# Attention: the order of the compressed parts of tiles 4 to 7, and the oldest key tile of tile 4's selected part

## The reference, cut to what matters

```python
o_cmp, o_sel = map_query_blocks(
    lambda q, p: nsa_cmp_sel(q, p, kc, vc, c_end, ks_b, vs_b, m_ov, rel_bias), (q_a,), pos)
...
o_win = window_attend(q_a..., band(kv_a[:, :, 4]), band(kv_a[:, :, 5]), k_pos, rel_bias)
o_lat = map_query_blocks(lambda ql, qr, p: mla_attend(ql, qr, ckv, k_rope, p, pos), (q_lat, q_rope), pos)
...
o_a = gates[..., 0:1] * o_cmp + gates[..., 1:2] * o_sel + gates[..., 2:3] * o_win
```

## Time and profile before

| | |
|---|---|
| median of 3 runs | 1113.71 us (1111.62 to 1114.09) |
| profiled execution | 1115.21 us |
| its span | 1113.2 us |
| busy: TensorE, VectorE, ScalarE, GpSimd | 1075.2, 624.6, 362.5, 86.5 us |
| granted TensorE clock, mean | 0.991 of 2.4 GHz |
| attention of the prompt | from about 386 to 753 us |

### The profile page before, as it was taken

The page is one execution under the profiler, slowest core; times in us unless marked ns, Lnnn a source line. Parts: engine busy times, 40 slices in busy tenths (PEclk is TensorE's granted clock), DMA queues, the critical chain, the costliest instruction groups (busy, mean ns, idle before and its releaser), DMA issues. The chain is left out here.

```text
span 1113.2 us, 22587 instructions
## 1 busy us (share of the span) xinstructions
PE 1075.2 (97%) x8368; PEld 763.3 (69%) x8368; DVE 624.6 (56%) x1627; ACT 362.5 (33%) x893; POOL 86.5 (8%) x184
## 2 busy tenths in 40 slices
PE   6899999999999999998999999999999999999997
PEld 3455599998886677776776657664544576777775
DVE  0645323463423477769677766742323588888883
ACT  0322001121112475546555555631112133333330
POOL 0210100110000011101101010011000200000000
PEclk9899999999999999999999999999999999999998
DMA  9933270001006240000000000005794467878781
GB/s 355 310 115 94 72 211 2 16 19 72 1 1 122 44 116 2 1 1 2 1 2 1 2 1 2 1 1 119 169 307 152 142 217 262 271 274 275 261 251 51
DMA packets 96612, 120.25 MB, mean 108 GB/s; under 512 B 31569, under 2 KB 65380, under 8 KB 95480
## 3 DMA queue, kind: packets, MB, share of 16 engines
q1 hardware_dynamic: 96504, 118.81, 34.4%
HBM read 104.41 MB, written 14.36 MB: 107 GB/s over the span
## 5 line engine op out<-in xcount | busy, mean ns | idle before, releaser
L549 PE MATMUL PS<-AR 128*128 128x256 f32 (+2 forms) x896 | 219.7, 403 | 0.0
L549 PEld LDWEIGHTS PS<-AR 128*128 128x128 f32 x896 | 167.8, 190 | 45.2 <-issue 6.2
L2090 PE MATMUL PS<-AR 128*128 128x512 f32 x256 | 112.3, 592 | 0.0
L1747 PE MATMUL PS<-CA,AR 128*128 128x128 f32 x704 | 111.4, 282 | 0.8 <-ACT AR L1821 0.8
L963 DVE TENSOR_TENSOR AR<-PS,AR 128x256 f32<-128x256 f32 (+2 forms) x80 | 36.2, 452 | 134.4 <-PE PS L549 134.3
L1747 PEld LDWEIGHTS PS<-CA,AR 128*128 128x128 f32 x704 | 77.0, 143 | 44.6 <-issue 31.7
L1821 ACT ACTIVATE AR<-PS 128x512 f32<-128x512 f32 (+1 forms) x108 | 58.2, 546 | 125.1 <-PE PS L1747 124.5
L1725 PE MATMUL PS<-AR 128*128 128x65 f32 (+1 forms) x688 | 89.3, 271 | 0.0
L2090 PEld LDWEIGHTS PS<-AR 128*128 128x128 f32 x256 | 47.5, 190 | 54.0 <-issue 54.0
L1725 PEld LDWEIGHTS PS<-AR 128*128 128x128 f32 x688 | 84.3, 192 | 0.0
L1806 ACT ACTIVATE AR<-PS,SM_ 128x512 f32<-128x512 f32 (+4 forms) x192 | 76.6, 471 | 15.9 <-DVE SM_ L1914 8.8
(11 more groups left out here) (364 smaller groups left out, 1622.9 us busy)
## 6 DMA issues: line engine op xcount, KB each, us to landing
AR<-in_cache_nsa SPq DMA_DIRECT2D x128, 256.0 KB, 5.0
AR<-in_cache_mla SPq DMA_DIRECT2D x128, 96.0 KB, 3.7
AR<-in_x_prompt SPq DMA_DIRECT2D x16, 512.0 KB, 4.6
AR<-in_w_ada SPq DMA_DIRECT2D x3, 2048.0 KB, 11.4
AR<-in_w_in SPq DMA_DIRECT2D x6, 1024.0 KB, 8.4
AR<-in_w_ada SPq DMA_DIRECT2D x8, 512.0 KB, 4.3
AR<-in_w_out SPq DMA_DIRECT2D x4, 1024.0 KB, 10.0
AR<-in_w_out SPq DMA_DIRECT2D x2, 2048.0 KB, 17.5
```

The lines of the kernel that those rows point to most:

```text
L549: mm = pe.matmul(bank[:, 0:WIDE[g]], tokens[:, k, :], w, start=(fresh and k == 0), stop=(last and k == 3), skip_group_check=True)
L1747: mm = pe.transpose(PS[:, 4 + c % 2, P * (t - t0):P * (t - t0) + P], tile(u, t), ident)
L2090: mm = pe.matmul(PS[0:n, 2 + 2 * (m % 2) + c, :], YTO[m % 2][:, f, 0:n], weights[:, f, 512 * c:512 * c + 512], start=(f == 0), stop=(f == 7))
```

## The change

It does three things. The compressed part of each of the tiles 4 to 7 comes directly before that tile's local part; the order of the stages is then compressed, local, selected, latent. The selected part of tile 4 gets an `old` unit of its own for its oldest key tile, as the local parts have, so its other four units have 4 key tiles and one slot each. For this the functions ask `apart(kind, i)` where they asked for a local part. And the selected part of tile 4 becomes crossed like its neighbours. In `oldest` this part needs no mask, so its scores are copied; the copy waits for the exponentials of every earlier part that reads the same third of `BTX`.

```diff
-        STAGES += [(i, "cmp") for i in range(4, NT)] + [(i, kind) for i in range(4, NT) for kind in ("win", "sel", "mla")]
+        STAGES += [(i, kind) for i in range(4, NT) for kind in ("cmp", "win", "sel", "mla")]
         UNITS, GROUPS = [], []
+
+        def apart(kind, i):
+
+            return kind == "win" and i >= 4 or kind == "sel" and i == 4
+
...
-            if kind == "win" and i >= 4:
+            if apart(kind, i):
                 UNITS.append(("old", i, 0, [(r, g) for r in range(R) for g in range(G)], k0, 1, len(GROUPS)))
...
-            if nb > 4 and kind != "win":
+            if nb > 4 and not apart(kind, i):
                 SLOTS.append((0, 1))
...
-        TURNS_BACK = [kind == "sel" and i >= 5 or kind == "win" and i >= 4 for kind, i, half, last in GROUPS]
+        TURNS_BACK = [kind in ("sel", "win") and i >= 4 for kind, i, half, last in GROUPS]
...
-                        keys = KSELT if kind == "sel" else KWINT
+                        keys = KSELT if GROUPS[og][0] == "sel" else KWINT
...
-                    sc = BTX[:, R * g + r, 256:384] if kind == "win" and lo else PSF[:, o + lo:o + hi]
+                    sc = BTX[:, R * g + r, 256:384] if apart(kind, i) and lo else PSF[:, o + lo:o + hi]
...
-                past = [v for v in WHOLE if UNITS[v][0] == "win" and UNITS[v][1] == i - 1] if i > 4 else []
+                past = [v for v in WHOLE if v < u and apart(*UNITS[v][0:2])]
                 if past:
                     dve.wait_ge(s_exp, EXP0[past[-1] + 1])
                 kept = BTX[:, :, 256:384].rearrange("p (g r) c -> p g r c", g=G)
...
+                sc = scores(u, 0, 0, 1024).rearrange("p (g r c) -> p g r c", g=G, c=P)
+                if GROUPS[og][0] == "sel":
+                    ins = dve.tensor_copy(kept, sc)
+                else:
+                    ins = dve.tensor_tensor(kept, sc, wmask.rearrange("p (g r c) -> p g r c", g=1, r=1)
+                                            .to_broadcast([P, G, R, P]), ALU.add)
+                ins.then_inc(s_old, 1)
                 dve.wait_ge(s_old, sum(OLD[:u + 1]))
                 oldest_minima(0)
```

More of the change, by code:

```diff
@@ L1847, in oldest @@
                 kept = BTX[:, :, 256:384].rearrange("p (g r) c -> p g r c", g=G)
-                dve.tensor_tensor(kept, scores(u, 0, 0, 1024).rearrange("p (g r c) -> p g r c", g=G, c=P),
-                                  wmask.rearrange("p (g r c) -> p g r c", g=1, r=1).to_broadcast([P, G, R, P]), ALU.add)\
-                    .then_inc(s_old, 1)
+                sc = scores(u, 0, 0, 1024).rearrange("p (g r c) -> p g r c", g=G, c=P)
[5 more added lines that the diff above has]
+                ins.then_inc(s_old, 1)
                 dve.wait_ge(s_old, sum(OLD[:u + 1]))
@@ L1867, in extremes @@
                 nm = NM[:, NTH[u] % 2, 0:len(heads)]
-                kept = kind == "win" and i >= 4
+                kept = apart(kind, i)
                 near = {"cmp": 64, "mla": P, "sel": min(256, P * nb), "win": min(256, P * nb)}[kind]
```

## The result

The changed kernel takes 1124.3 us (median of 6 runs, 1123.7 to 1129.62) where the kernel before took 1111.52 us beside it: the ratio is 1.0116, with a 95% interval of 1.0095 to 1.0137. I had forecast slower, 1117.0 us, and 1120.8 us as the upper end. A second comparison on another occasion gave 1124.56 us against 1114.36 us (17 runs of before), ratio 1.0088 [1.0066, 1.0109].

What follows compares the result with a forecast made beforehand. TensorE, busy for 1075.2 of 1113.2 us, was taken as the bound. Terms -1.2 - 1.1 + 6.1 - 0.5 = +3.3 us gave 1117.0 us on the median of 1113.71 us, range 1112.3 to 1120.8 us.

Steps and rivals of the forecast that it cites:

- (c): Entries into local parts of tiles 5 to 7: cover gone, two pauses each; 6.1 us more, bounds 2.5 and 8.5.
- (d): Selected part of tile 4: TensorE's work falls 1.0 us, about 0.5 us of new pauses; 0.5 us less in sum.
- (a): Compressed parts of tiles 5 to 7 leave the run: three 1.62 us steps become 1.21 us; 1.2 us less.
- (b): Entry into tile 4's local part: first pause 0.8 us in place of 1.95, second stays 1.2; 1.1 us less.
- full exposure: Upper bound on new pauses in tile 4's selected part: VectorE's copy, two minima and a wait, 3.2 us; 1119.7 us.
- the one I named for (d): Rival: tile 4's selected part runs on VectorE, copy and two minima with 3.2 us exposed; 1119.7 us, chance 0.16.
- Covered entries: Rival: each of the four entries into local parts costs at most 0.41 us; sum -4.0 us, 1109.7 us, chance 0.13.
- no second pause: Rival: first compressed group finished in time at entries, 2.4 to 4.8 us below forecast; 1112.2 to 1114.6 us, chance 0.16.
- The clock rival: Clock falls at three new entries into local parts, 2.3 us each, giving 1124 us; chance 0.03.

Runs made afterwards that it cites:

- e1: Kernel before with only the stage order changed: compressed parts of tiles 4 to 7 each lead their local part; 1121.88 us against 1113.9, ratio 1.0073.
- e10: e2 with one exchange on ScalarE: eviction of the last local unit's first chunk before the first selected exponentials; 1112.81 against 1113.79 us, ratio 0.9995.
- e8: Kernel before with the run of compressed parts of tiles 4 to 7 moved before tile 3's latent part; 1109.61 against 1114.36 us, ratio 0.9954.
- e9: Kernel before with the compressed part of tile i + 4 behind that of tile i, for tiles 0 to 3; 1108.34 against 1113.79 us, ratio 0.9944.
- e2: Changed kernel with the stages in the old order, so only tile 4's selected part is changed; 1117.91 us, ratio 1.0035.
- e5: Kernel before with tiles 4 to 7 in the order local, compressed, selected, latent; 1128.03 us, ratio 1.0127.
- e4: e2 with a place of its own in SBUF for the copy of the selected part's oldest tile; 1117.12 us, ratio 1.0026.
- e6: Kernel before with only tile 7's compressed part leading its local part; 1113.57 against 1113.79 us, ratio 1.0006.
- e7: e1 with the second late finish ahead of the third unit's minimum on VectorE at entries into tiles 4 to 7; 1121.44 us, ratio to before 1.0061.
- e3: Kernel before with tile 4's selected part crossed, both slots per unit, no unit for its oldest tile; 1113.2 against 1113.9 us, ratio 0.9996.

## Why the prediction was wrong

The direction was right, and so was the place and cause of the largest term (c); the size was 3.3 us where 9.9 us came in the stage. Term (d) was forecast as 0.5 us of gain and was a loss of 3.6 us (9.9 less the 6.3 of e1), which makes 4.1 of the 6.6 us that are missing. By its own steps:

(a) The steps of 1.62 us went, worth 1.2 us. Right. (b) The first pause at tile 4 became 0.73 us, 0.8 forecast. The second became 1.73 us where I had kept it at 1.2. This is the step that failed in (b) and for tile 6 in (c). I took the second pause from the old entry, but it is counted from the second unit's scores, and the latent values that cover the first pause stand ahead of these. With 0.5 us lost there (b) was worth 0.6 us, not 1.1.

(c) "The pause is 3.1 - 1.85 = 1.25 us" measured 1.18, and 1.2 us for the second measured 1.29. The pauses were right to 0.1 us at tiles 5 and 7. What the sum lacked was 0.5 us of the second pause at tile 6, 1.6 us of TensorE's own work at the three entries (put at nothing; 0.4 us of each are the scores in smaller batches), and the 0.68 us before tile 5's compressed scores. Forecast 6.1 us, measured 9.0 us (3.3 + 3.1 + 2.6), of which 0.7 us belongs to (d).

(d) "Following the order at these durations I get about 0.5 us of new pauses" is the step that made the forecast wrong. 4.1 us came (4.3 in place of 0.2), over the bound of 3.2 us that I had called full exposure. I followed VectorE's list and TensorE's, and not ScalarE's: there the eviction of an old chunk stands behind the first exponentials of the new part. My bound summed VectorE's own added work, but a wait that passes through three engines in strict order is not bounded by the added work of one. e10 shows it: one exchange on ScalarE leaves 0.20 us of the 2.78. The local part, which I took as the pattern for the lower end, has no such wait: its addition starts with no idle time in front of it, the copy after 3.15 us. Nor is the addition the larger work: 1.22 us against 1.23 us for the copy. TensorE's saving of 1.0 us was real: from tile 4's first crossed values to its latent scores it is busy for 24.6 us in place of 25.8.

The rivals: the one I named for (d) had the place right and the engine and size wrong. "Covered entries" and "no second pause" are refuted by the changed kernel and e1, which have both pauses at all four entries. The clock rival I gave 0.03 and dismissed because one trace kept its clock through two pauses. In the profiled execution of the changed kernel it kept it too; in others it did not.

## What to carry to other kernels

Where every engine works its list in strict order, as in this kernel, follow a moved or added wait through the lists of all of them: the costly thing is what stands behind the waiting instruction on an engine that one has not looked at, here an old eviction behind new exponentials. Light parts (little TensorE work, full VectorE and ScalarE chains) took the cover from local and selected units that followed them, and hardly from latent ones (e8, e9), so put them in front of heavy parts of a simple kind, a few at a time, and not in front of the parts with the longest chain. Before counting work as cover for two pauses in a row, look whether it also stands ahead of the work from which the chain of the second one starts; then it only moves that pause.

## What the runs showed of the hardware

I had not expected how often the granted clock falls inside this stage. It is 1.00 throughout in the traces of the kernel before and of the changed one, and not in others of the same code. Busy time by stretch of the second execution of the changed kernel, around its pause of 2.79 us (columns as in the earlier trace rows):

```profile
528.00:531.00 3.00, 0.84 (x13) 0.60 (x12) 2.39 (x8) 1.45 (x5) 0.73 (x1) 0.95 0.00 0
531.00:534.00 3.00, 2.38 (x12) 1.52 (x14) 0.42 (x1) 1.24 (x5) 0.00 (x0) 0.50 0.00 0
534.00:537.00 3.00, 3.00 (x9) 0.69 (x5) 1.53 (x5) 0.10 (x1) 0.00 (x0) 0.50 0.00 0
```

The same stretch of the first execution, with a pause of 2.78 us:

```profile
527.00:530.00 3.00, 0.70 (x12) 0.46 (x10) 2.25 (x7) 1.59 (x5) 0.72 (x1) 1.00 0.00 0
530.00:533.00 3.00, 2.52 (x18) 1.30 (x18) 0.84 (x2) 1.10 (x5) 0.00 (x0) 1.00 0.00 0
```

In the one the clock is 0.50 behind the pause, the level of 1.2 GHz, in the other it stays at 2.4 GHz. The second's stage is 379.1 us, 1.7 us longer. The same happened in e2 behind its pauses of 1.95 and 2.78 us, in e5 behind 2.29 and 2.66 us, in e4 and e6 behind 1.95 us, and in e2, e4, e6, e7 and e9 behind the pause of 1.2 us at the start of the attention stage. In e7 it also fell behind the pauses of 1.21 and 0.46 us at tile 5 (0.62 from 578 to 579 us, 0.50 behind that), and in e4, e6 and e10 just behind the end of the stage, after two pauses of 0.91 and 0.88 us (in e10 0.64 from 756 to 757 us, 0.50 behind that). Two of these stretches of e2, the same view, behind the pause at the start and behind the one of 1.95 us:

```profile
390.00:393.00 3.00, 3.00 (x17) 2.54 (x16) 0.94 (x6) 1.58 (x6) 0.00 (x0) 0.50 1.05 205
525.00:528.00 3.00, 3.00 (x14) 2.11 (x11) 2.85 (x11) 2.97 (x12) 0.00 (x0) 0.59 0.00 0
```

It did not happen behind 1.95 us in e3 and e10, nor behind 2.05 and 2.60 us in e5, and the pause at the start left it at 1.00 in eight of the thirteen traces. So pauses of 0.9 to 2.8 us stood ahead of every fall in this stage and just behind it, and the same pauses often left the clock as it was; what decides between the two, no run here shows. The Trainium skill, page "TensorE: Matmul & The Clock Gate", section "A second HAM failure mode: psum-queue depth-cycling", says that frequent small idle gaps between groups of matmuls make the clock swing. The trace of before, which I had held against it, stays at 1.00 behind 1.95 and 1.17 us; of the later traces some fall behind such pauses and some do not, so they agree in part.

This also bears on the scatter of the kernel before (1110.65 to 1119.64 us in 19 runs), which goes with the clock in part: the three fastest had 0.991 to 0.993, the two slowest 0.982, but five of 1115.1 to 1115.8 us had 0.991 or 0.992 too. e8 and e9 have fewer long pauses, and gain 4.8 and 5.4 us in the median. For e9 the stage accounts for some 4 us of that. For e8 it accounts for 0.9 us; the mean granted clock of its runs was 0.9936 beside 0.9896, which points to the clock for the rest. That is argued from averages: I made no run that changes the clock alone, and where the rest of these gains comes from stays open.
